# Closing contraction chunks done token tile by token tile, and a fused final scale, in a two-layer diffusion step

## The reference

```python
# trunk_layer, for both groups of tokens
h = rmsnorm(x, g_attn) * (1 + scale1) + shift1
... # input projection, Fourier, attention and pooling branches, gates
x = x + gate1 * ((gf * branch_f + ga * branch_a + gp * branch_p) @ w_out)
h2 = rmsnorm(x, g_ffn) * (1 + scale2) + shift2
x = x + gate2 * peer_ffn(h2, peer_wq, peer_keys, peer_u, peer_v)
# after the last layer
y = rmsnorm(x, g_final)

# peer_ffn: 16384 experts, 8 heads x 16 chosen per token
act = gelu(peer_u[chosen] . h)       # "first table"
out = sum(g * act * peer_v[chosen])  # "second table"
```

## Time and profile before

| | us |
|---|---|
| median of 3 runs (lowest, highest) | 3430.69 (3430.19, 3432.68) |
| the profiled execution | 3435.16 |
| its span, first to last instruction | 3433.2 |
| PE busy | 3277.9 (95%) |
| DVE busy | 2046.7 (60%) |
| ACT busy | 1014.2 (30%) |
| POOL busy | 1004.0 (29%) |
| mean granted TensorE clock | 0.979 of full speed |

### The profile page before, as it was taken

How to read it: one execution, slowest core, us unless ns; L and a number is a source line. 1 busy time by engine, 2 the same in 40 slices (tenths; PEclk the granted TensorE clock), 3 DMA queues, 4 the chain that set the end, 5 groups by cost and what they waited for, 6 DMA issues and landing times.

```text
span 3433.2 us, 47500 instructions
## 1 busy us (share of the span) xinstructions
PE 3277.9 (95%) x16498; PEld 2778.2 (81%) x16498; DVE 2046.7 (60%) x4132; ACT 1014.2 (30%) x1348; POOL 1004.0 (29%) x434
## 2 busy tenths in 40 slices
PE   8898989999999999999997989899999999999997
PEld 1576665499999998888886767689999999888886
DVE  0345458900399937777754464599059964777775
ACT  0222222233344332222222222233343433222221
POOL 0442341255534340000005424446553443000000
PEclk9999999999999999999998999999999999999998
DMA  8723334645466675665644323234456667565562
GB/s 287 243 92 105 104 110 148 236 168 177 172 210 208 210 271 214 226 232 214 227 161 144 111 80 107 102 122 173 169 187 204 214 207 265 221 239 217 225 233 88
DMA packets 252712, 628.70 MB, mean 183 GB/s; under 512 B 26768, under 2 KB 130768, under 8 KB 231760
## 3 DMA queue, kind: packets, MB, share of 16 engines
q1 hardware_dynamic: 240944, 619.79, 51.4%
q10 hardware_dynamic: 11680, 7.78, 0.8%
HBM read 524.20 MB, written 107.06 MB: 184 GB/s over the span
## 4 chain that ended last, share of the span: by engine, by line
issue 77%; POOL 22%; POOLq 1%; DMA 0%; DVE 0%; DVEq 0%
POOL wlo L538 21%; POOLq L537 0%; POOL rstd L534 0%; POOLq L533 0%; POOLq L550 0%; DMA u<-in_g_final 0%; DVE x L1464 0%; POOLq L542 0%; DVEq L1465 0%; DVE z L1097 0%; POOLq L141 0%; POOLq L546 0%; DVEq L1086 0%; POOLq L554 0%; DVE nhalf L1082 0%
## 5 line engine op out<-in xcount | busy, mean ns | idle before, releaser
L538 POOL TENSOR_TENSOR wlo<-raw,whi 128x1024 fp32r<-128x1024 f32 x400 | 987.8, 2472 | 1247.2 <-ACT whi L601 645.9
L1010 PE MATMUL acc<-lt_hi,whi 128*128 128x384 f32 x2048 | 696.3, 340 | 8.6 <-POOL wlo L538 8.6
L1010 PE MATMUL acc<-lt_lo,whi 128*128 128x384 f32 x2048 | 687.4, 336 | 0.0
L1010 PE MATMUL acc<-lt_hi,wlo 128*128 128x384 f32 x2048 | 687.0, 335 | 0.0
L1036 PE MATMUL acc<-whi,bt_lo 128*128 128x512 f32 x1536 | 597.9, 389 | 0.0
L1036 PE MATMUL acc<-whi,bt_hi 128*128 128x512 f32 x1536 | 597.9, 389 | 0.0
L1036 PE MATMUL acc<-wlo,bt_hi 128*128 128x512 f32 x1536 | 597.9, 389 | 0.0
L695 ACT ACTIVATE whi<-raw 128x1024 fp32r<-128x1024 f32 x256 | 271.6, 1061 | 748.0 <-PE acc L1036 748.0
L1430 DVE TENSOR_TENSOR wlo<-raw,whi 128x1024 fp32r<-128x1024 f32 x256 | 316.0, 1235 | 243.7 <-ACT whi L695 243.7
L1407 DVE TENSOR_SCALAR u<-iota,u 128x128 f32<-128x128 f32 x768 | 398.3, 580 | 42.9 <-issue 31.7
L1010 PEld LDWEIGHTS acc<-lt_hi,whi 128*128 128x128 f32 x2048 | 386.4, 189 | 8.9 <-issue 8.9
(11 more groups left out here) (149 smaller groups left out, 3421.4 us busy)
## 6 DMA issues: line engine op xcount, KB each, us to landing
raw<-in_ut SPq DMA_DIRECT2D x128, 1024.0 KB, 5.0
raw<-in_peer_v SPq DMA_DIRECT2D x128, 1024.0 KB, 4.8
raw<-in_w_ada SPq DMA_DIRECT2D x96, 512.0 KB, 4.9
acts<-u SPq DMA_DIRECT2D x128, 384.0 KB, 2.3
gmat<-u SPq DMA_DIRECT2D x48, 1024.0 KB, 5.1
z<-gmat SPq DMA_DIRECT2D x32, 1536.0 KB, 7.9
u<-acts SPq DMA_DIRECT2D x32, 1536.0 KB, 8.2
raw<-in_w_gate SPq DMA_DIRECT2D x24, 1024.0 KB, 5.1
```

The costliest lines, as they stand in the source:

```text
L538: pool.tensor_tensor(wlo[:, slot], raw[:, slot], whi[:, slot].bitcast(F32), ALU.subtract).then_inc(lo_ready, 1)
L1010: mm = pe.matmul(acc[j][:, 0:T], w[:, j, c * P:(c + 1) * P], x[:, c, :], start=(c == 0 and q == 0), stop=(c == KC - 1 and q == 2))
```

## The change

The output projection's last four units (`U_OUT`+4 to +7) no longer run one after the other through all tiles. After the last transposition and all waits for chunks, `by_tile` goes tile by tile: for each tile the four units, both halves. It closes tile 0's banks, then tile 1's, then tile 2's, and gives all four weight slots back at the end. The second table's last four keys are done in the same way. `residual` waits for the banks in the order t, h. At the end of the last layer DVE makes the result straight from `X`, the root and `GFIN` in one instruction for each tile, `GFIN` lies at another place in `U` and is loaded during the last layer's first table, and each tile is stored when it is done.

```diff
-        GFIN = part(0, D)
+        GFIN = part(10240, D)
...
+                        if last:
+                            sp.dma_start(GFIN, a["g_final"].to_broadcast([P, D])).then_inc(gfin_landed, 16)
...
-            sp.wait_ge(layer_free, DEPTH + 1)
-            sp.dma_start(GFIN, a["g_final"].to_broadcast([P, D])).then_inc(gfin_landed, 16)
-            sp.wait_ge(y_ready, 1)
-            sp.dma_start(o["y_prompt"], X[:, 0, :]).then_inc(y_stored, 16)
-            sp.dma_start(o["y_sample"].rearrange("(b p) n -> p b n", p=P), X[:, 1:3, :]).then_inc(y_stored, 16)
+            for t in range(TB):
+                sp.wait_ge(y_ready, t + 1)
+                out = o["y_sample"][(t - 1) * P:t * P, :] if t else o["y_prompt"]
+                sp.dma_start(out, X[:, t, :]).then_inc(y_stored, 16)
...
+                def by_tile(u0, lt, chunk, use):
+
+                    for t in range(TB):
+                        for i in range(SLOTS):
+                            if t == 0:
+                                pe.wait_ge(lo_ready, l * LOS + u0 + i + 1 + SLOTS)
+                            s = (u0 + i) % SLOTS
+                            lh, ll = (x[:, chunk + i, t * P:(t + 1) * P] for x in lt)
+                            for h in range(2):
+                                for n, (x, w) in enumerate(((lh, whi), (lh, wlo), (ll, whi))):
+                                    mm = pe.matmul(accum(use + TB * h + t)[:], x, w[:, s, h * HB:(h + 1) * HB],
+                                                   start=False, stop=(i == SLOTS - 1 and n == 2))
+                                if i == SLOTS - 1:
+                                    mm.then_inc(acc_done, 1)
+                    pe.drain().then_inc(unit_used, SLOTS)
+
                 def turned_pass(src, base, ready, u0, use, ht0):
+                    late = KC - SLOTS if u0 == U_OUT else KC
                     for k in range(KC + 3):
                         if k < KC:
                             ready(k)
                             turn(src, base, k)
                         if k >= 3:
                             pe.wait_ge(ht_ready, l * (3 * KC) + ht0 + k - 2)
-                            unit(u0 + k - 3, (LTh, LTl), k - 3, use, k == 3, k == KC + 2)
+                            if k - 3 < late:
+                                unit(u0 + k - 3, (LTh, LTl), k - 3, use, k == 3, k == KC + 2)
+                    if late < KC:
+                        by_tile(u0 + late, (LTh, LTl), late, use)
...
-                for j in range(8):
-                    retrieve(KEYS // 8 - 1, j, False, j == 7)
+                for j in range(8 - SLOTS):
+                    retrieve(KEYS // 8 - 1, j, False)
+                for t in range(TB):
+                    for j in range(8 - SLOTS, 8):
+                        if t == 0:
+                            pe.wait_ge(vlo_ready, l * KEYS + KEYS - 8 + j + 1 + SLOTS)
+                            pe.wait_ge(w_ready, l * KEYS + KEYS - 8 + j + 1)
+                        wh, wl = (x[:, j, t * P:(t + 1) * P] for x in (BTh, BTl))
+                        for h in range(2):
+                            for q, (x, w) in enumerate(((wh, whi), (wh, wlo), (wl, whi))):
+                                mm = pe.matmul(accum(C_V + TB * h + t)[:], x, w[:, j % SLOTS, h * HB:(h + 1) * HB],
+                                               start=False, stop=(j == 7 and q == 2), skip_group_check=True)
+                            if j == 7:
+                                mm.then_inc(acc_done, 1)
+                pe.drain().then_inc(unit_used, SLOTS)
...
-                            dve.tensor_tensor(XTMP[:, n % 2], accu(use + TB * h + t)[:], gates[:, min(t, 1), h * HB:(h + 1) * HB],
+                            dve.wait_ge(acc_done, l * ACCS + use + 2 * t + h + 1)
+                            dve.tensor_tensor(XTMP[:, n % 2], accum(use + TB * h + t)[:], gates[:, min(t, 1), h * HB:(h + 1) * HB],
                                               ALU.mult).then_inc(acc_free, 1)
...
                 residual(C_V, GATE2)
-                normalise(l * 2 + 3)
-                dve.drain().then_inc(xn_ready, 1)
-                dve.sem_inc(layer_free, 1)
+                if not last:
+                    normalise(l * 2 + 3)
+                    dve.drain().then_inc(xn_ready, 1)
+                    dve.sem_inc(layer_free, 1)
...
             for t in range(TB):
-                dve.tensor_tensor(X[:, t], XN[:, t], GFIN, ALU.mult)
-            dve.drain().then_inc(y_ready, 1)
+                dve.wait_ge(rstd_ready, 2 * DEPTH * TB + t + 1)
+                dve.scalar_tensor_tensor(X[:, t], X[:, t], rstd[:, t:t + 1], GFIN, ALU.mult, ALU.mult).then_inc(y_ready, 1)
```

More of the change, by code:

```diff
@@ L513, in _ @@
             layer(DEPTH - 1, True)
-            sp.wait_ge(layer_free, DEPTH + 1)
-            sp.dma_start(GFIN, a["g_final"].to_broadcast([P, D])).then_inc(gfin_landed, 16)
-            sp.wait_ge(y_ready, 1)
-            sp.dma_start(o["y_prompt"], X[:, 0, :]).then_inc(y_stored, 16)
-            sp.dma_start(o["y_sample"].rearrange("(b p) n -> p b n", p=P), X[:, 1:3, :]).then_inc(y_stored, 16)
+            for t in range(TB):
+                sp.wait_ge(y_ready, t + 1)
+                out = o["y_sample"][(t - 1) * P:t * P, :] if t else o["y_prompt"]
+                sp.dma_start(out, X[:, t, :]).then_inc(y_stored, 16)
             sp.wait_ge(kv_stored, 32 * DEPTH)
-            sp.wait_ge(y_stored, 32)
+            sp.wait_ge(y_stored, 16 * TB)
         @block.gpsimd
@@ L1022, in chosen, with retrieve @@
                     mm.then_inc(aux_done, 1)
-                def retrieve(i, j, first, last):
+                def retrieve(i, j, first):
                     m = i * 8 + j
@@ L1036, in retrieve @@
                                 mm = pe.matmul(accum(C_V + b)[:], x, w[:, j % SLOTS, h * HB:(h + 1) * HB],
[L1037 to L1040, removed]
+                                               start=(first and q == 0), stop=False, skip_group_check=True)
+                    mm.then_inc(unit_used, 1)
                 for j in range(SLOTS):
@@ L1065, in layer @@
                 for j in range(8):
-                    retrieve(0, j, j == 0, False)
+                    retrieve(0, j, j == 0)
                 with pe.Fori(1, KEYS // 8 - 1) as i:
                     for j in range(8):
-                        retrieve(i, j, False, False)
-                for j in range(8):
-                    retrieve(KEYS // 8 - 1, j, False, j == 7)
+                        retrieve(i, j, False)
+                for j in range(8 - SLOTS):
[13 more added lines that the diff above has]
+                pe.drain().then_inc(unit_used, SLOTS)
             pe.wait_ge(silu_ready, 1)
```

## The result

The changed kernel takes 3440.17 us (median of 9 runs, 3438.34 to 3443.32) beside 3430.9 for the kernel before on the same chip. The ratio is 1.0028, with a 95% interval of 1.0018 to 1.0038: slower by 9.6 us (6.2 to 13.0). The forecast was 3439.6, or 8.9 slower. One execution of the last kernel of the experiments ran at a mean clock of 0.554 and took 5518.32 us; it is left out of that kernel's numbers.

A forecast was written before the change was run, and what follows sets the result against it. TensorE works nearly the whole span, so only its waits count. Losses 2 x (5.3 + 2.5 + 4.5) minus gains 3.5 and 12.2 give +8.9 us: 3439.6 on the median, range 3434.0 to 3445.5.

The forecast's parts named there:

- Table border: Between the layers, the second table's tile order brings TensorE's transposition 3.5 us earlier (bounds 2.5 to 3.9).
- Rival 3: At the second table no tile is really ahead, the 3.5 us go at both places: +15.9, 3446.6 us; chance 0.08.
- The end: Kernel's end: span ends 10.6 us after the last multiply's start instead of 22.8, gain 12.2 (10.0 to 12.9).
- the cover: Layer 1's first table: splits in TensorE's slots hide the early scale load; cost nothing, without them up to 2.6 us.
- Chunk 7: Output projection, each layer: TensorE waits for chunk 7's low half before the units by tile, 5.3 us lost.
- Half clock: Output projection, each layer: after standing still about 5 us TensorE runs at half clock, 2.5 us lost (1.5 to 2.8).
- Rival 1: In the output projection the closing units pay but the clock stays up: +3.9, 3434.6 us; chance 0.13.
- Tail: Behind each output projection, roots stand behind GpSimd's four late splits, delaying the transposition: 4.5 us lost (3.7 to 5.6).
- Behind that nothing changes: After the tail, the next pass loses nothing more: its first four units' weights are ready and later loads aren't wanted yet.
- Rival 2: The projections' losses are given back later in the layer, at an unmoved wait; all back gives -15.7, 3415.0 us; chance 0.05.

The follow-up runs named there:

- the last kernel of the experiments: The changed kernel with transpositions further ahead, squares and roots before the next splits, GpSimd's second to fourth split held for the first chunk: 3408.27 us, 0.9934 of before.
- two units, new order: The changed kernel with only the last two projection units by tile, squares and roots ahead of the two late splits: 3409.18 us, ratio 0.9940 to before.
- the same with GpSimd waiting: As two units, new order, but GpSimd holds the two late splits until the first chunk is ready: 3405.21 us, ratio 0.9932 to before.

## Why the prediction was right, step by step

The sum was right, and four of its five terms were within 0.2 us of their places. That the total came as near as 0.7 was in part luck (last point).

- **Table border**: 3.5 predicted, 3.46 measured. Rival 3 (no tile really ahead) falls: the transposition came 6.52 behind the last multiply instead of 9.98.
- **The end**: L+10.6 predicted, L+10.69 measured, 12.2 against 12.13. GpSimd's power was held, 1.41 instead of 0.55, as in the row on which the term rested, though VectorE's product there had one tensor less to read. The last scaling began at L+6.33 (predicted L+6.3) and took 1.28 (1.17). The scale's load did disturb its neighbour: ScalarE waited 5.66 for the weights (first row below) where it waited 4.29, yet TensorE has no wait from there to the end of the second table; the cover held.
- **Chunk 7**: 5.3 predicted, 5.42 measured, of which 5.17 is the wait (5.18 in layer 0); giving the lead back took it away.
- **Half clock**: this is the term that was mis-sized. At its place it cost 1.42 (1.37 in layer 0), under the lower bound of 1.5, not 2.5; in two other kernels with the same wait it was 1.51 to 1.59. I took the length of the slow stretch from the nearest row, 5.4 us; here it was about 3. Rival 1 (no half clock; the prediction calls it the second in one place) falls all the same: the clock was 0.50, and with the wait gone it was 1.00.
- **Tail**: 4.5 predicted, 15.93 - 11.39 = 4.54 measured, with GpSimd's start at L+1.66 (L+1.67) and the last root's end at L+15.06 (L+15.1). That it was the order of the splits, and no other engine, is shown by moving them.
- **"Behind that nothing changes"** failed. Layer 1 lost 1.78 more behind the tail (1.9 in the output projection alone), by the clock again. Layer 0 lost about 1.3, as shown below the rows. So the sum came out near by luck: 1.1 too much in the clock term of each layer, 2.2 in all, stood against 3.1 left out. Rival 2 (given back later) falls: nothing came back.

Four bounds of the prediction don't follow from the numbers beside them: the table's 2.5 and 3.9 would be 2.1 and 4.2, the tail's 3.7 and 5.6 would be 3.4 and 5.2. The measured places lie inside either set.

ScalarE's wait in the kernel after; then stretches behind the border to the next pass, of the kernel after and of the one before (the columns as above):

```profile
2889.01 1.06 ACT L687 ACTIVATE whi<-raw 128x1024 fp32r<-128x1024 f32 x1 [5.66 <-DMA raw<-in_ut]
```

```profile
2183.95:2189.60 5.65, 5.65 (x13) 4.49 (x14) 1.59 (x4) 0.00 (x0) 0.00 (x0) 0.51 0.00 0
2279.80:2286.00 6.20, 6.20 (x22) 6.20 (x23) 5.98 (x38) 1.53 (x2) 6.20 (x3) 0.57 0.48 154
```

```profile
2170.60:2174.10 3.50, 3.50 (x8) 2.82 (x9) 1.60 (x4) 0.00 (x0) 0.00 (x0) 0.50 0.44 179
2265.60:2271.80 6.20, 6.20 (x27) 6.20 (x28) 5.98 (x38) 1.72 (x3) 6.20 (x3) 0.72 0.41 157
```

After the change 13 multiplies went at half clock in the first stretch, before 8; and at the next wait (4.44 us in both) the clock stood at 0.57 over the stretch, before at 0.72. Each is worth about 0.9. In layer 0 too the first 18 multiplies behind the border took longer, 6.82 us instead of 5.93. From the next pass's first unit to the second table's last multiply, layer 0 took 1330.3 to 1330.9 us in the three kernels that begin that pass at L+20.7, and 1329.0 to 1329.5 in the six changed ones that begin it at L+16.1 or L+16.2. The execution of the kernel before took 1331.5, because it lost 2.1 us in a part of the stretch that the change doesn't touch, and so hides this when only two traces are compared. With some 1.3 for it the stretches make 8.4 + 1.3 = 9.7 without that scatter, beside the measured 9.6.

## What to carry to other kernels

When a loop is turned so that one output is finished early, look at what the old order handed back piece by piece: inputs wanted one at a time, buffers freed one at a time. Turn only as many steps as there is lead on both sides, here two units, or four once their inputs are fetched earlier, and then check what the engines that free up do next, since work queued ahead of the critical step in a fixed program order moves to the wrong side of it. Price a loss that stands at a place from the timelines and add it up place by place; that held here within 0.2 us, while the clock's share didn't.

## What the hardware showed unexpectedly

The half-clock stretch does not follow the length of the stop ahead of it. Take a stop from a pass's last multiply to the next pass's first, with a few transpositions in between, and call a multiply slow that took over 0.5 us. Behind the output projection, 13 multiplies were slow after a stop of 20.7 us (the kernel after), 8 after 16.2 (before), 7 after 12.9 (two units, new order) and 11 after 11.3 (the same with GpSimd waiting). Between the layers the stop was 16.3 in every kernel with the new table order, and yet 6 multiplies were slow there in the kernel without the projection's part and 14 in the one with the table alone. The Trainium skill (TensorE: Matmul & The Clock Gate, section HAM oscillation — how this bites in real kernels) describes a kernel in which each group of matmuls behind a wait starts at the lower clock; the groups behind all these stops started at half clock too. How long it lasts stays open here, at about 1.5 us of uncertainty for a stop.

The same load can take far longer among others than alone. The scale's 512 KB took 3.5 us from issue to landing at the end of the kernel before, with nothing beside it, and 12.3 in the kernel after, behind gate rows and between weight pairs (DMA issues: count, KB each, us from issue to landing; before, then after):

```profile
u<-in_g_final SPq DMA_DIRECT2D x1, 512.0 KB, 3.5
```

```profile
u<-in_g_final SPq DMA_DIRECT2D x1, 512.0 KB, 12.3
```

Over those 12.3 us the 16 DMA engines were busy throughout (the last three numbers: clock, DMA share, GB/s):

```profile
2873.70:2886.00 12.30, 12.30 (x73) 12.30 (x72) 7.27 (x9) 3.38 (x5) 5.43 (x3) 1.00 1.03 398
```
